# Seven products of quarters for the value projections of two mixers, in one place

## The chip, the cores and the metric

The kernel runs on one core of one Trainium2 chip. The metric is the device time of one execution in microseconds, the median of the timed runs. A core has TensorE (PE, matrix products; its loads of the stationary operand are listed as PEld), VectorE (DVE), ScalarE (ACT), GpSimd (POOL) and SyncE (SP). Each engine works through its own list of instructions in order, and the lists are tied together by semaphores: an instruction can wait until a semaphore has a value, and can raise one when it is done. SP, ACT and POOL also issue DMAs.

## The reference, cut to what matters

One layer of a decoder on 512 tokens of width 1024: a norm, one input projection `w_in`, four token mixers that run beside each other, a gated sum, an output projection, and a gated MLP. The part at issue is the projection of the normed x onto the values of two of the mixers, 512 columns each:

```
xn = rmsnorm(x, mix_norm_g[l])
p = xn @ w_in[l]
(aq, ak, av, ao, ai, af, bb, bc, bx, cz, cxbc, cdt,
 sq, sk, sv, gates) = jnp.split(p, SPLIT_POINTS, axis=-1)
ya = mlstm(aq, ak, av, ao, ...)
yd = stick_breaking_attention(sq, sk, sv)
```

So `[sv | av]` = xn (512 x 1024) times a matrix of 1024 x 1024. `sv` are the values of the stick-breaking attention (called D in the kernel, four heads), `av` those of the mLSTM (A, four heads). C is the Mamba-2 mixer, whose convolved input is `xbc`; B is the short convolution.

## The kernel before

**Precision.** Each product of two float32 matrices is made of three matmuls in the format fp32r: high by high, high by low, low by high. ACT makes the high part of a weight tile (`w_hi`, L862, a copy that rounds), DVE the low part (`w_lo`, L1262, source less high part). The same is done for activations (`xn_hi`, `xn_lo`).

**Units.** The weights come as a stream of units. A unit is one tile of 128 x 1024 floats (512 KB), and an ordinary one gives one output tile of 128 columns by 512 tokens: 8 steps over the inner dimension, 24 matmuls with 512 moving columns. SP loads unit u + 4 into `raw`, a ring of four, when `lo_ready` says that unit u's raw tile has been read. In ACT's list iteration u waits for the end of unit u on TensorE (`unit_done`) and makes `w_hi` of unit u + 4 first; then come the evacuation of unit u and the steps that other mixers hang on it. DVE's iteration u makes `w_lo` of unit u + 4 first, then the same. Since the lists are in order, whatever stands behind a wait is held with it.

**Order of units.** D's q (0 to 3) and k (4 to 7), D's values (`U_DV`, 8 to 11), the small gates (`U_SMALL` = 12), A's q and k (13 to 16), A's values (`U_AV`, 17 to 20), A's output gate (21 to 24), xbc of C (`U_XBC`, 25 to 32), gates and lifts (from `U_GL_D` = 33), z, B, and so on, then the output projection (from 97) and the MLP.

**The two value projections.** They are wanted with tokens on the partitions, so the x tile is the stationary operand and the weights move. D's values (L516) run in four units over four PSUM banks, 96 matmuls of 512 columns. A's values (L534) run in four units, half the columns at a time, 192 matmuls of 256 columns. DVE copies them to `dv` (L1332) and `av` (L1336).

**PSUM.** Eight banks, GB0 to 3 and X0 to 3. Units 4 to 7 go to X1, X2, X3, X0.

**The stick-breaking heads.** Head h starts at unit `D_AT[h]` = 12 + 4h. On TensorE: scores at that unit's end (L626), the suffix sums at the end of the third unit after (L652, waits for `sp_lo`), the product with the values at the fourth (L640). Between them DVE masks (L1437), ACT makes abs, exp and ln over 1280 columns (L985 to L987), DVE adds (L1442), ACT makes `sp_hi` (L991), DVE `sp_lo` (L1273); after the suffix DVE subtracts (L1419) and ACT makes exp (L961); after the product ACT makes `y_hi` (L978) and DVE `y_lo`, which raises `d_lo`.

**The mLSTM heads** start at unit 33 (`A_AT`). Their first scores (L671) wait for all four heads' `d_lo`.

**The xbc units.** ACT scales the tile into `stg` with the last tap (L926), DVE adds three taps (L1354), ACT makes the silu of the tile before (L933). In the sixth of them that silu waits for all sixteen `d_suffix`. Silu, exp/ln and sigmoid are in different tables, and a change of table is a load (L850).

**The start.** ACT makes the rstd of x by unit 2; POOL multiplies x_in by it (L415); ACT and DVE make `xn_hi` and `xn_lo`, with the gain folded in, beside units 3 to 6.

**The down projection** at the end already uses seven products of quarters, with the quarters' sums of its weights made by accumulating DMAs that POOL issues (L471), and the sums of its activations by DVE (L1711 to L1718).

Of the kernel before, what the change touches and what calls it, by code (L numbers as in the profile page):

```python
# [26 lines left out]
ALU = mybir.AluOpType  # L27
# [4 lines left out]
P = 128  # L32
# [36 lines left out]
PRODUCTS = ("P1", "P5", "P6", "P3", "P7", "P2", "P4")  # L69
# [7 lines left out]
C_T = 52  # L77
# [31 lines left out]
def build(nc, w_stream, w_quad, xT, vecs, rowsm, finrow, out_tok):  # L109
# [18 lines left out]
    bank_of = [o % 8 if o < 8 else o % 4 if o < 12 else o % 3 if o < first_tile[U_OUT] else (o + BANK0) % 4 for o in range(TILES0)]  # L128
# [129 lines left out]
    def low(name, offset):  # L258
# [14 lines left out]
    x1_turned = at("x1_turned", [P, KD, T], F32, TURNED)  # L273
    xg, st = at("xg", [P, NB, T], F32, base), f_ac
# [5 lines left out]
    Q11, Q12, Q21, Q22 = range(4)  # L280
    PLAIN_ORDER = (0, 1, 4, 5, 2, 3, 6, 7)
# [15 lines left out]
        dv_done d_scores d_masked d_soft_in d_soft d_sp_hi d_sp_lo d_suffix d_expo d_weights d_out d_hi d_lo  # L297
# [56 lines left out]
    def _(sp):  # L354
# [52 lines left out]
    def _(pool):  # L407
# [6 lines left out]
        for k in range(KD):  # L414
# [11 lines left out]
        pool.wait_ge(S["unit_done"], U_DV)  # L426
        pool.memset(negm[:], 0.0).then_inc(S["filled"], 1)
        pool.memset(g_x[:], 0.0).then_inc(S["masks"], 1)
        pool.memset(g_row[:], 0.0).then_inc(S["masks"], 1)
        pool.wait_ge(S["masks"], 5)  # L430
        pool.wait_ge(S["filled"], 4)
        pool.affine_select(out=negm[:], in_=negm[:], compare_op=ALU.is_ge, fill=NEG, base=-1,
                           pattern=[[1, T]], channel_multiplier=-1).then_inc(S["masks"], 1)
        pool.wait_ge(S["unit_done"], U_SMALL + 1)
# [45 lines left out]
    def _(pe):  # L480
# [23 lines left out]
        def unit(u):  # L504
# [3 lines left out]
            if U_DV <= u < U_DV + 4:  # L508

                part = u - U_DV  # L510
                for tb in range(NB):
                    if part == 0:
                        bank_free(o + tb)
                    for k in range(2):
                        for q, (x, w) in enumerate(((xn_hi, w_hi), (xn_lo, w_hi), (xn_hi, w_lo))):
                            ins = pe.matmul(GB[tb][:, :], x[:, 2 * part + k, tb * P:tb * P + P],  # L516
                                            w[:, u % RING, k * T:k * T + T], start=(part == 0 and k == 0 and q == 0),
                                            stop=(part == 3 and k == 1 and q == 2))
                    if part == 3 and tb < NB - 1:
                        ins.then_inc(S["dv_done"], 1)  # L520
                ins.then_inc(S["unit_done"], 1)
                return
            if U_AV <= u < U_AV + 4:


                half = (u - U_AV) % 2
                for tb in range(NB):
                    if half == 0 and tb % 2 == 0:
                        bank_free(o + tb // 2)
                    out = gb(o + tb // 2)[:, 256 * (tb % 2):256 * (tb % 2) + 256]  # L530
                    for k in range(4):
                        c = k * 256
                        for q, (x, w) in enumerate(((xn_hi, w_hi), (xn_lo, w_hi), (xn_hi, w_lo))):
                            ins = pe.matmul(out, x[:, 4 * half + k, tb * P:tb * P + P], w[:, u % RING, c:c + 256],  # L534
                                            start=(half == 0 and k == 0 and q == 0 and tb % 2 == 0),
                                            stop=(half == 1 and k == 3 and q == 2), skip_group_check=True)
                ins.then_inc(S["unit_done"], 1)
                return
# [46 lines left out]
        for u in range(U_OUT):  # L585
# [25 lines left out]
            if u == 22:  # L611
# [1334 lines left out]
```

## Time and profile before

| | us |
|---|---|
| median of 3 runs | 999.82 |
| lowest, highest | 999.6, 999.83 |
| profiled execution | 999.67 |
| its span | 997.9 |
| TensorE busy in it | 990.7 |
| DVE busy | 648.1 |
| ACT busy | 449.7 |
| POOL busy | 46.0 |

The profiled execution is one run; what lies outside its span is 1.8 us. A busy TensorE is made of matmuls that overlap: each row of a 512-column matmul lasts 0.39 us, but the next one starts earlier. So durations of stretches on TensorE are taken from start to start.

### The profile page before, as it was taken

The page shows a single profiled execution, that of the slowest core. Times are in us where ns is not written, and L with a number is a line of the kernel's source. Part 1 is how long each engine was busy: PE and PEld are TensorE (multiplying, and loading weights), DVE is VectorE, ACT ScalarE, POOL GpSimd, SP SyncE. Part 2 cuts the span into 40 slices and gives each one's busy share as a digit, 9 for nine tenths or more (in the row PEclk, how much of TensorE's full clock was granted, in tenths as well). Part 3 has the DMA queues.
Part 4 walks back from the last instruction along what each step waited for, and adds up shares of the span by engine and source line. Part 5 has one row for each costly group of instructions (what it writes and reads, how often), then busy time and mean ns, then how long its engine had stood idle before and what let it go on. Part 6 is the DMA issues. An engine that isn't in the chain of part 4 may idle for free.

```text
span 997.9 us, 12378 instructions
## 1 busy us (share of the span) xinstructions
PE 990.7 (99%) x4520; PEld 811.5 (81%) x4520; DVE 648.1 (65%) x869; ACT 449.7 (45%) x561; POOL 46.0 (5%) x64
## 2 busy tenths in 40 slices
PE   9999999999999999999999999999999999999997
PEld 7878988888787887777888888888888888888886
DVE  6836753757777566556463447767777777764775
ACT  7424455555645322444332334454444444442646
POOL 0610000000000000000000000000000000001210
PEclk9999999999999999999999999999999999999999
DMA  7332221223322343442252332274232232367942
GB/s 255 124 112 85 85 87 64 85 95 105 106 82 78 131 132 116 138 135 88 86 187 88 104 96 95 86 169 125 84 105 92 97 105 84 104 237 199 196 86 85
DMA packets 49002, 115.08 MB, mean 115 GB/s; under 512 B 20276, under 2 KB 21428, under 8 KB 48832
## 3 DMA queue, kind: packets, MB, share of 16 engines
q1 hardware_dynamic: 27072, 91.62, 27.3%
q0 software_dynamic: 5008, 20.51, 8.2%
q10 hardware_dynamic: 16880, 2.37, 1.5%
q8 instruction: 29, 0.48, 0.2%
q14 instruction: 13, 0.11, 0.0%
HBM read 110.24 MB, written 4.25 MB: 115 GB/s over the span
## 4 chain that ended last, share of the span: by engine, by line
PE 96%; DVE 1%; ACT 1%; issue 1%; DMA 0%; SPq 0%; ACTq 0%
PE gb L486 71%; PE xb L788 5%; PE gb L788 2%; PE xb L486 2%; PE gb L516 2%; PE gb L534 2%; PE gb L768 2%; PE xb L768 2%; PE xb L652 1%; PE gb L569 1%; PE xb L724 1%; PE xb L626 1%; PE gb L640 1%; PE xb L682 1%; PE gb L833 1%
## 5 line engine op out<-in xcount | busy, mean ns | idle before, releaser
L1262 DVE TENSOR_TENSOR w_lo<-raw,w_hi 128x1024 fp32r<-128x1024 f32 x152 | 189.3, 1245 | 208.1 <-ACT w_hi L862 207.6
L862 ACT ACTIVATE w_hi<-raw 128x1024 fp32r<-128x1024 f32 x153 | 161.9, 1058 | 323.4 <-PE gb L486 283.8
L486 PE MATMUL gb<-xn_hi,w_hi 128*128 128x512 f32 x720 | 282.0, 392 | 0.0
L486 PE MATMUL gb<-xn_hi,w_lo 128*128 128x512 f32 x720 | 280.3, 389 | 0.0
L486 PE MATMUL gb<-xn_lo,w_hi 128*128 128x512 f32 x720 | 280.2, 389 | 0.0
L486 PEld LDWEIGHTS gb<-xn_hi,w_hi 128*128 128x128 f32 x720 | 135.2, 188 | 28.4 <-issue 0.8
L486 PEld LDWEIGHTS gb<-xn_hi,w_lo 128*128 128x128 f32 x720 | 135.2, 188 | 28.4
L486 PEld LDWEIGHTS gb<-xn_lo,w_hi 128*128 128x128 f32 x720 | 135.3, 188 | 27.8 <-issue 0.2
L486 PE MATMUL gb<-y_hi,w_hi 128*128 128x512 f32 x352 | 138.4, 393 | 0.0
L486 PE MATMUL gb<-y_hi,w_lo 128*128 128x512 f32 x352 | 137.0, 389 | 0.0
L486 PE MATMUL gb<-y_lo,w_hi 128*128 128x512 f32 x352 | 137.0, 389 | 0.0
L486 PEld LDWEIGHTS gb<-y_hi,w_hi 128*128 128x128 f32 x352 | 66.1, 188 | 14.6 <-issue 0.9
L486 PEld LDWEIGHTS gb<-y_lo,w_hi 128*128 128x128 f32 x352 | 66.0, 188 | 14.2 <-issue 0.7
L486 PEld LDWEIGHTS gb<-y_hi,w_lo 128*128 128x128 f32 x352 | 66.1, 188 | 13.9
L850 ACT ACT_TABLE_LOAD x35 | 44.9, 1283 | 5.6 <-DVE t L1525 3.7
L1753 DVE TENSOR_TENSOR w_lo<-wr,w_hi 128x1024 fp32r<-128x1024 f32 x24 | 28.9, 1223 | 25.3 <-ACT w_hi L1179 25.3
L1179 ACT ACTIVATE w_hi<-wr 128x1024 fp32r<-128x1024 f32 x24 | 25.2, 1059 | 38.1 <-PE gb L768 15.6
L1128 ACT ACTIVATE f_cv<-f_sq,vec 128x512 f32<-128x512 f32 x40 | 32.4, 809 | 16.2 <-DVE f_sq L1691 16.2
L1691 DVE TENSOR_TENSOR f_sq<-gb,f_rs 128x512 f32<-128x512 f32 x40 | 27.6, 689 | 16.8 <-PE gb L486 16.1
L1697 DVE SCALAR_TENSOR_TENSOR f_cv<-f_sq,vec,f_cv 128x510 f32<-128x510 f32 x40 | 30.0, 750 | 6.1 <-DVE f_cv L1694 6.1
L1694 DVE SCALAR_TENSOR_TENSOR f_cv<-f_sq,vec,f_cv 128x511 f32<-128x511 f32 x40 | 29.9, 749 | 1.0
L1138 ACT ACTIVATE a_hi<-f_cv 128x256 f32 x16 | 6.7, 417 | 40.7 <-DVE f_cv L1702 40.7
(308 smaller groups left out, 1268.2 us busy)
## 6 DMA issues: line engine op xcount, KB each, us to landing
raw<-w_stream SPq DMA_DIRECT2D x153, 512.0 KB, 3.3
wr<-w_quad POOLq DMA_DIRECT2D x16, 512.0 KB, 7.3
abc<-scr_a POOLq DMA_DIRECT2D x8, 640.0 KB, 4.1
wr<-w_quad SPq DMA_DIRECT2D x8, 512.0 KB, 5.3
x_in<-xT SPq DMA_DIRECT2D x8, 256.0 KB, 5.4
x<-xT POOLq DMA_DIRECT2D x1, 2048.0 KB, 8.5
scr_x<-x_turned ACTq DMA_DIRECT2D x4, 512.0 KB, 5.7
x<-scr_x POOLq DMA_DIRECT2D x1, 2048.0 KB, 16.4
```

Of the source, the lines that this page charges most:

```text
L486: ins = pe.matmul(out, w[:, r, lo:hi], rhs(k)[x], start=(first and n == 0 and q == 0), stop=(last_ and n == len(ks) - 1 and q == 2))
L768: ins = pe.matmul(DOWN_PS[n][:, :], x[:, k, tt * P:tt * P + P], w[:, (U_DOWN + k) % RING, fh(h)], start=(k == 0 and q == 0), stop=(k == N_ ...
L788: ins = pe.matmul(ps[tau][:, :], x[:, p, tau * P:tau * P + P], w[:, r, fh(half)], start=(first and q == 0), stop=(last_ and q == 2), skip_ ...
L850: act.preload_act_table_set(name)
L862: act.activation(w_hi[:, r, 0:n], raw[:, r, 0:n], ACT.Copy).then_inc(S["hi_ready"], 1)
L1128: act.activation(f_cv[:, half, side, :], f_sq[:], ACT.Identity, bias=fcw[:, tile, 3:4], scale=fcw[:, tile, 2:3]).then_inc(S["f_tap"], 1)
L1179: act.activation(w_hi[:, u % RING, :], src, ACT.Copy).then_inc(S["hi_ready"], 1)
L1262: dve.tensor_tensor(w_lo[:, r, 0:n], raw[:, r, 0:n], w_hi[:, r, 0:n].bitcast(F32), ALU.subtract)\
L1691: dve.tensor_tensor(f_sq[:], ps[:, :], f_rs[:], ALU.mult).then_inc(S["psum_read_dve"], 1)
L1694: dve.scalar_tensor_tensor(out=w[:, 1:T], in0=f_sq[:, 0:T - 1], scalar=fcw[:, tile, 1:2], in1=w[:, 1:T], op0=ALU.mult, op1=ALU.add).then_i ...
L1697: dve.scalar_tensor_tensor(out=w[:, 2:T], in0=f_sq[:, 0:T - 2], scalar=fcw[:, tile, 0:1], in1=w[:, 2:T], op0=ALU.mult, op1=ALU.add).then_i ...
L1753: dve.tensor_tensor(w_lo[:, u % RING, :], source(name, j), w_hi[:, u % RING, :].bitcast(F32), ALU.subtract)\
```

## The change

It computes `[sv | av]` in one place, unit 8 on, as a product of two matrices cut into quarters (tokens 2 x 256, inner dimension 2 x 512, columns `sv` and `av`), with seven products of quarters where a plain one has eight. Each product is 24 matmuls with 512 moving columns and takes two units, so the section has 14 units (8 to 21), in the order P1, P2, P5, P3, P6, P7, P4.
- Weights: `wv` holds the first quarter and POOL adds others to it by three accumulating DMAs for each half; `wv2` likewise, once. P2's quarter comes through the ring. ACT and DVE make high and low parts for all 14.
- Activations: at the end of unit 7 ACT multiplies x_in by the gain, in eight pieces. DVE makes four sums (`v_a5`, `v_s2`, `v_s4`, `v_s3`, 128 x 1024 each), and ACT and DVE split each into high and low.
- Results: P1 stays in its banks, and P6, P7, P4 are added onto it there; ACT copies intermediate results to `dv` and `av`, and DVE adds or subtracts onto them.
- TensorE waits for DVE's read of unit 7 ahead of the section.
- The small gates become unit 22; w_small no longer carries the gain, as x_in does. A's values as units of their own are gone. The D heads start at 22, 26, 30, 34; xbc is 31 to 38; `U_GL_D` is 39. All later units move by six, with the same distances among them. The counts of semaphores that the down projection shares are raised, and SP's list is adapted.

The core of the diff; the first `values` is TensorE's, the gained x is in ACT's iteration 7, the second `values` is DVE's:

```diff
+V_PRODUCTS = ("P1", "P2", "P5", "P3", "P6", "P7", "P4")
+U_DQ, U_DK, U_V = 0, 4, 8
+U_SMALL = U_V + 2 * len(V_PRODUCTS)
+SKIP = U_SMALL - U_V - 2
+U_AQ, U_AK, U_AO, U_XBC = U_SMALL + 1, U_SMALL + 3, U_SMALL + 5, U_SMALL + 9
+U_GL_D = U_XBC + 8
-D_AT = [12 + 4 * h for h in range(D_HEADS)]
-A_AT = [33 + 4 * h for h in range(A_HEADS)]
+D_AT = [U_SMALL + 4 * h for h in range(D_HEADS)]
+A_AT = [U_GL_D + 4 * h for h in range(A_HEADS)]
...
+        def v_add(tile, j, q, name, sem):
+            pool.wait_ge(S["lo_ready"], V_OF[name] + j + 1)
+            pool.dma_start(tile[:, j, :], v_quad[q, j], accum_op=ALU.add).then_inc(S[f"{sem}{j}"], 16)
...
+        def values():
+            pe.wait_ge(S["xn_ready"], KD)
+            pe.wait_ge(S["psum_read_dve"], order[first_tile[U_V - 1]][1])
+            for name in V_PRODUCTS:
+                u = V_OF[name]
+                fresh = name in ("P1", "P2", "P5")
+                if name in ("P1", "P2", "P3"):
+                    if name == "P3":
+                        pe.wait_ge(S["s_lo"], 2)
+                    for j in range(2):
+                        pe.wait_ge(S["lo_ready"], u + j + 1)
+                        for tau in range(2):
+                            if name == "P3" and j == 0:
+                                pe.wait_ge(S["v_put"], 3 + tau)
+                            for kk in (2 * j, 2 * j + 1):
+                                ins = v_step(name, kk, tau, fresh and kk == 0, kk == 3)
+                        ins.then_inc(S["unit_done"], 1)
+                    continue
+                pe.wait_ge(S["s_lo"], {"P5": 1, "P6": 3, "P7": 4, "P4": 4}[name])
+                pe.wait_ge(S["lo_ready"], u + 1)
+                for tau in range(2):
+                    if name == "P6" and tau == 0:
+                        pe.wait_ge(S["v_put"], 2)
+                    elif name == "P7":
+                        pe.wait_ge(S["s_read"], 3 + tau)
+                    elif name == "P4":
+                        pe.wait_ge(S["s_read"], 5 + tau)
...
+            if u == U_V - 1:
+                act.wait_ge(S["xn_ready"], KD)
+                for k in range(KD):
+                    act.activation(x_in[:, k, :], x_in[:, k, :], ACT.Identity, scale=gain(V_MIX, k))\
+                        .then_inc(S["v_gained"], 1)
...
+        def values():
+            dve.wait_ge(S["v_gained"], KD)
+            dve.tensor_tensor(v_a5[:], xq(4, 1), xq(0, 1), ALU.subtract).then_inc(S["f_s2"], 1)
+            dve.wait_ge(S["f_s2"], 1)
+            dve.scalar_tensor_tensor(out=v_s2[:], in0=v_a5[:], scalar=-1.0, in1=xq(0, 0),
+                                     op0=ALU.mult, op1=ALU.subtract).then_inc(S["f_s2"], 1)
+            v_lo_of(12)
+            dve.wait_ge(S["f_s2"], 2)
+            dve.scalar_tensor_tensor(out=v_s4[:], in0=xq(4, 0), scalar=-1.0, in1=v_s2[:],
+                                     op0=ALU.mult, op1=ALU.subtract).then_inc(S["f_s2"], 1)
+            dve.tensor_tensor(v_s3[:], xq(0, 0), xq(0, 1), ALU.subtract).then_inc(S["f_s2"], 1)
+            v_lo_of(13)
+            v_split(0)
+            v_split(1)
+            v_lo_of(14)
+            v_split(2)
+            v_split(3)
+            dve.wait_ge(S["unit_done"], V_OF["P2"] + 2)
+            dve.wait_ge(S["v_put"], 2)
+            for tau in range(2):
+                dve.tensor_tensor(dv[:, tau, :], dv[:, tau, :], V_A[tau][:, :], ALU.add).then_inc(S["s_read"], 1)
+            for u in range(15, 20):
+                v_lo_of(u)
+            for tau in range(2):
+                dve.wait_ge(*((S["unit_done"], V_OF["P6"] + 2) if tau else (S["o_part"], 2)))
+                dve.wait_ge(S["v_put"], 5 + tau)
+                dve.scalar_tensor_tensor(out=av[:, tau, :], in0=V_B[tau][:, :], scalar=-1.0, in1=av[:, tau, :],
+                                         op0=ALU.mult, op1=ALU.subtract).then_inc(S["s_read"], 1)
...
```

ACT's list in the section, in words: `w_hi` of unit 12 after the gained x, `w_hi` 13, two copies of P1, the splits `v_h5` and `v_h4`, `w_hi` 14, the splits `v_h2` and `v_h3`, `w_hi` 15, the copy of P5's first half, `w_hi` 16, the copy of its second half, `w_hi` 17, `w_hi` 18 (waits for wv2's first half with its accumulating load), the copies of the masks, `w_hi` 19 (second half), the two copies of P3, `w_hi` 20 to 25 and the last two copies. Of the wv2 loads, POOL issues the first when `w_lo` 14 is done and the second when `w_lo` 15 is.

## Rows read from the trace of the kernel before

**Rows 1.** page: busy times, clock granted to TensorE, chain that ended last
```profile
PE 990.7 (99%) x4520; PEld 811.5 (81%) x4520; DVE 648.1 (65%) x869; ACT 449.7 (45%) x561; POOL 46.0 (5%) x64
PEclk9999999999999999999999999999999999999999
PE 96%; DVE 1%; ACT 1%; issue 1%; DMA 0%; SPq 0%; ACTq 0%
```

**Rows 2.** waits of TensorE: engine, line <- releaser: us, times, longest
```profile
PE xb L565 <- POOL cst L410: 1.1, 1, 1.1
```

**Rows 3.** timeline of TensorE (start, us, line, what): first values, behind them
```profile
51.24 0.39 PE L516 MATMUL gb<-w_hi,xn_hi 128*128 128x512 f32 x1
...
73.10 1.92 PE L555 MATMUL gb<-x_in,w_small 128*32 128x512 f32 x16
```

**Rows 4.** timeline of TensorE: the second mixer's values, 106 to 134 us
```profile
106.92 0.36 PE L534 MATMUL gb<-w_hi,xn_hi 128*128 128x256 f32 x1
...
124.65 0.40 PE L652 MATMUL xb<-sp_hi,tri_r 128*128 128x512 f32 x1
...
127.36 0.33 PE L534 MATMUL gb<-w_hi,xn_hi 128*128 128x256 f32 x1
...
133.16 1.67 PE L626 MATMUL xb<-dq,dk 128*128 128x512 f32 x4
```

**Rows 5.** timelines of ACT and DVE at the end of unit 7
```profile
51.44 1.06 ACT L862 ACTIVATE w_hi<-raw 128x1024 fp32r<-128x1024 f32 x1 [4.38 <-PE xb L486]
...
52.54 1.23 DVE L1262 TENSOR_TENSOR w_lo<-raw,w_hi 128x1024 fp32r<-128x1024 f32 x1 [1.57 <-ACT w_hi L862]
53.68 0.68 DVE L1325 TENSOR_TENSOR dk<-xb,stg 128x512 f32<-128x512 f32 x1
```

**Rows 6.** timelines: gained x on ACT; a quarter's piece, two splits, DVE
```profile
11.35 2.78 ACT L889 ACTIVATE y_hi<-x_in,vec 128x512 fp32r<-128x512 f32 x4
...
867.70 0.42 DVE L1714 SCALAR_TENSOR_TENSOR s<-a,f_cv 128x256 f32 x1
...
930.59 2.35 DVE L1273 TENSOR_TENSOR l<-s,h 128x1024 fp32r<-128x1024 f32 x2
```

**Rows 7.** accumulating loads by POOL, all sixteen: time to landing
```profile
DMA to landing us min/median/max: 5.2/7.3/9.7
```

**Rows 8.** the same, of the one issued at 902.3 us alone
```profile
DMA to landing us min/median/max: 5.5/5.5/5.5
```

**Rows 9.** TensorE: fourth head's scores, suffix, values; first mLSTM scores
```profile
162.55 2.32 PE L626 MATMUL xb<-dq,dk 128*128 128x512 f32 x8
...
183.24 0.39 PE L652 MATMUL xb<-sp_hi,tri_r 128*128 128x512 f32 x1
...
191.46 2.32 PE L640 MATMUL gb<-t,dv 128*128 128x512 f32 x8
...
220.94 0.48 PE L671 MATMUL xb<-aq,ak 64*128 64x256 f32 x1
```

**Rows 10.** timeline of DVE: sp_lo, subtraction, an xbc evacuation, y_lo
```profile
181.16 1.49 DVE L1273 TENSOR_TENSOR sp_lo<-t,sp_hi 128x1280 fp32r<-128x1280 f32 x1 [1.34 <-ACT sp_hi L991]
...
187.07 1.67 DVE L1419 TENSOR_TENSOR t<-t,xb 128x512 f32<-128x512 f32 x4
192.17 2.32 DVE L1354 SCALAR_TENSOR_TENSOR stg<-gb,vec,stg 128x511 f32<-128x511 f32 x3 [3.43 <-ACT stg L926]
...
197.76 0.68 DVE L1273 TENSOR_TENSOR y_lo<-gb,y_hi 128x512 fp32r<-128x512 f32 x1
```

**Rows 11.** timeline of ACT: softmax's first step; table load, tap, silu
```profile
168.98 1.27 ACT L985 ACTIVATE t<-t 128x1280 f32<-128x1280 f32 x1
...
190.07 1.28 ACT L850 ACT_TABLE_LOAD   x1
191.36 0.78 ACT L926 ACTIVATE stg<-gb,vec 128x512 f32<-128x512 f32 x1
192.04 0.62 ACT L933 ACTIVATE xbc<-stg 128x512 f32<-128x512 f32 x1
```

More of the change, by code:

```diff
@@ L273, in build, with v_op @@
     x1_turned = at("x1_turned", [P, KD, T], F32, TURNED)
+    wv = at("wv", [P, 2, 1024], F32, A0 + 6 * 4 * T)
+    wv2 = at("wv2", [P, 2, 1024], F32, C0)
+    def v_op(name, dt, offset):
+        return at(name, [P, 4, 2 * P], dt, offset)
+    T0_AT, Y0_AT, OP = G0 + 3 * 4 * 4 * T, G0 - 8 * 4 * T, 4 * 2 * P * 4
+    v_a5, v_s2 = v_op("v_a5", F32, T0_AT), v_op("v_s2", F32, T0_AT + OP)
+    v_s4, v_s3 = v_op("v_s4", F32, Y1 + 4 * 4 * T), v_op("v_s3", F32, Y1 + 4 * 4 * T + OP)
+    v_l5, v_l2 = v_op("v_l5", F32R, T0_AT), v_op("v_l2", F32R, T0_AT + OP)
+    v_l4, v_l3 = v_op("v_l4", F32R, Y1 + 4 * 4 * T), v_op("v_l3", F32R, Y1 + 4 * 4 * T + OP)
+    v_h5, v_h4, v_h2, v_h3 = (v_op(n, F32R, Y0_AT + q * OP) for q, n in enumerate(("v_h5", "v_h4", "v_h2", "v_h3")))
+    V_SPLIT = [(v_a5, v_h5, v_l5), (v_s4, v_h4, v_l4), (v_s2, v_h2, v_l2), (v_s3, v_h3, v_l3)]
     xg, st = at("xg", [P, NB, T], F32, base), f_ac
@@ L433, in _ @@
                            pattern=[[1, T]], channel_multiplier=-1).then_inc(S["masks"], 1)
+        for j in range(2):
+            v_add(wv, j, Q22, "P5", "wr_t")
+        for j in range(2):
+            v_add(wv2, j, Q12, "P3", "wr2_t")
+        for j in range(2):
+            v_add(wv, j, Q21, "P6", "wr_t")
+        pool.wait_ge(S["unit_done"], U_SMALL)
+        pool.memset(g_row[:], 0.0).then_inc(S["masks"], 1)
         pool.wait_ge(S["unit_done"], U_SMALL + 1)
@@ L507, in unit @@
             pe.wait_ge(S["lo_ready"], u + 1)
[L508 to L538, printed above, removed]
             for q in range(n):
@@ L1409, in _ @@
+        for u in range(U_OUT):
+            if U_V <= u < U_SMALL:
+                if u == U_V:
+                    values()
+                continue
+            if U_V - RING <= u < U_V:
+                v_lo_of(u + RING)
             elif u < U_OUT - 1:
@@ L1431, in _ @@
                 if h == 0:
[L1432 removed]
+                    dve.wait_ge(S["masks"], 5)
                 if h:
@@ L1865, in put @@
             stream[u + n] = slabs(w[:, n * width:(n + 1) * width])
-    def put_tokens(u, w):
-        for n in range(2):
-            s = slabs(w[:, 256 * n:256 * n + 256])
-            stream[u + 2 * n], stream[u + 2 * n + 1] = s[:, :1024], s[:, 1024:]
     put(U_DQ, sq); put(U_DK, sk);
-    for n in range(4):
-        stream[U_DV + n] = slabs(sv[256 * n:256 * n + 256])
+    both = (sv, av)
+    values = np.zeros((4, 2, P, 1024), np.float32)
+    for q in range(4):
+        for j in range(2):
+            k0 = 4 * (q // 2) + 2 * j
+            values[q, j] = slabs(both[q % 2][P * k0:P * k0 + 2 * P])
     small = np.zeros((D, P), np.float32)
```

301 lines of the change are left out of this document (201 added, 100 removed).

## The prediction

> **What bounds the kernel.** I read the page first: TensorE is busy for 990.7 of 997.9 us, and 96% of the chain that ended last is its matmuls [rows 1]. Of its waits for other engines the longest is 1.1 us, at the very start [rows 2]. So the time is the sum of TensorE's work, and every other engine counts only where TensorE would have to wait for it. A change is worth the TensorE time it removes less the stalls that it makes. Then I read the timeline of TensorE where the two value projections stand, and the timelines of DVE and ACT beside the steps that the change ties to them.
>
> **What is removed.** D's values run from 51.24 to 73.10: 21.86 us for 96 matmuls of 512 columns, so 0.2277 us each [rows 3]. A's values run from 106.92 to 133.16, with 2.71 us of another head's suffix matmuls between (124.65 to 127.36): 23.53 us for 192 matmuls of 256 columns [rows 4]. Together 45.39 us.
>
> **What is added on TensorE.** 7 products x 8 steps (4 tiles of the inner dimension, 2 of tokens) x 3 (high-high, high-low, low-high) = 168 matmuls of 512 columns, at 0.2277 us: 38.25 us. Without a stall the change would bring 7.1 us. Of that 5.5 come from the eighth product (24 x 0.2277), the rest from the 256-column form, which took more per column.
>
> **Stall 1, before P1.** The new code waits, ahead of all products, for DVE's read of unit 7, though P1 writes the banks of units 4 and 5. DVE's order is w_lo of unit 11 first, then the read; w_lo waits for w_hi, which ACT starts when unit 7 ends. Before, this ran beside D's values: w_hi at 51.44, w_lo 52.54, the read 53.68 to 54.36 [rows 5]. Now P1 starts at 54.42 in place of 51.24: 3.18 us. P1 then ends at 59.9 and P2 at 65.35, 24 matmuls or 5.46 us each.
>
> **Stall 2, before P5.** Its input is built from the gained x. ACT gains x only after w_hi of unit 11: from 52.40, eight pieces with 0.68 us between starts (four took 2.78), to 57.91 [rows 6]. DVE then does, in its order, v_a5, v_s2, w_lo 12, v_s4, v_s3, w_lo 13, v_l5: seven operations of 128x1024. Two such took 2.35 and so 1.15 each [rows 6], with 0.15 more where v_s2 waits for v_a5: v_l5 is there at 57.95 + 7 x 1.15 + 0.3 = 66.3. P5 waits 1.0 us, from 65.35 to 66.3. ACT's split of v_a5, 1.06 like a w_hi [rows 5], is done at 63.1 and hides. The new operations read x_in in four pieces of 256. If each piece cost as an operation of its own (0.42 in the down stage [rows 6], 1.7 for four), P5 would come 2 us later; a one-operation price is my value, as the split reads whole pieces too; below 1.15 nothing shows.
>
> **Behind P5.** P5 ends at 71.8, P3 at 77.2, P6 at 82.7, P7 at 88.2, P4 at 93.6. Against each stands: v_l4 at 67.4; the copy of P5's first half by ACT, 69.8; w_lo 15 at 73.2, needed at 74.4; w_lo 17 at 75.4. All in time. P7 has the least cover: it needs the first read of P6 by DVE, which is queued behind w_lo 19, behind w_hi 19, behind the accumulating load of wv2's second half. POOL issues that when w_lo 15 is done, at 73.2. The sixteen such loads of the down stage landed 5.2 to 9.7 us after their issue, 7.3 in the median [rows 7]; one that was alone took 5.5 [rows 8]. No plain load runs here (the ring's next slot waits for unit 22), and the two accumulating loads behind it come later, so I take 5.5: landed 78.7, w_hi 79.8, w_lo 81.0, read 81.7, needed 82.7. The end at 9.7 costs 3.2 us, below 6.5 it costs nothing. DVE's and ACT's other additions, the sel sums moved to the end of the section, and POOL's masks lie beside products and cost nothing.
> The section thus lasts 93.6 - 51.24 = 42.4 and gains 45.4 - 42.4 = 3.0 us.
>
> **What moves up.** The stick-breaking heads keep their distance of four units, but start nine units ahead of the first xbc unit (U_XBC) in place of thirteen. Before, only head 3 met xbc units, and its chain was already near TensorE's end of work: scores at 162.55, sp_lo done at 182.65, wanted at 183.24 [rows 9, 10]. Now head 2 has exactly this place, and head 3 follows four units on, between xbc units 3 and 7. I carry the times of before on (old unit 28 is new unit 34): scores of head 3 at T = 191.46.
> - DVE has an xbc evacuation and a w_lo ahead of the mask, which begins where y_lo began before, 197.76, and lasts as long as the subtraction, 1.7 [rows 10]; colT's copy now stands in this chain too and adds 0.2 net of the transposes that it waits for: 199.7. Before, softmax began at 168.98 and sp_lo ended at 182.65, 13.7 later [rows 10, 11]. Now 199.7 + 13.7 = 213.4. TensorE comes for it 20.7 after the scores, as before (162.55 to 183.24), at 212.1. Stall 3: 1.3 us.
> - Suffix (2.7) to 216.1. ACT, at xbc unit 5, now waits for the suffix of head 3 before a silu (before, it had long ended), and w_hi, DVE's w_lo and the subtraction, table load and exp come behind that: 0.2 + 0.6 + 1.0 + 1.2 + 1.7 + 1.3 = 6.0 [rows 5, 10, 11]. TensorE's unit 38 takes 5.5 (24 matmuls). Stall 4: 0.5 us.
> - A's first scores wait for y_lo of head 3. Before, that was done at 198.4 and A's scores stood at 220.94, with four units between [rows 9, 10]. Now y_lo is queued on DVE behind two xbc evacuations (2.3 each) and a w_lo, and on ACT behind table load, tap, w_hi, tap and two silus. From the exp's end: 1.3 + 0.8 + 2.3 + 1.15 + 2.3 + 0.6 + 0.5 + 0.65 = 9.6 [rows 10, 11], against 2.1 (weighted values, 2.32 less the tail that overlaps) + 5.5 (unit 39) on TensorE. Stall 5: 2.0 us.
> These are 3.8 us. Behind A's scores ACT and DVE stand to TensorE as before; all later units keep their distances.
>
> **The sum.** -3.0 + 3.8 = +0.8 on the profiled execution's 999.67, which lies 0.15 under the median of the timed runs: 1000.6.
>
> **The clock.** TensorE was granted its upper level, 2.4 GHz, in every slice, and no wait behind the start is as long as 1 us [rows 1, 2]. Stall 1 would be its first of 3 us, so the cost of an idle TensorE shows in no row. If one product's matmuls ran at the lower level, 1.2 GHz, they would take twice as long, 5.5 us more, of which stall 2's 1.0 absorbs a part: +4.5.
> The Trainium skill (TensorE: Matmul & The Clock Gate, Part 1) says that the array's clock is halved after idle time and given back only under sustained work. By that rule the sum could be 1005; by the trace, which has no such gap, it is 1000.6. No run here shows it yet.
>
> **Rivals.**
> 1. Forecast: both effects as worked out, 999 to 1001.8. Chance 0.53.
> 2. Heads hide: head 3's chain fits after all, stalls 3 to 5 vanish. For it: I assume that no step overlaps better than its queue order. Against: the A wait is explicit and its chain is built of rows. It decides at y_lo before the end of unit 39. 1000.6 - 3.8 = 996.8. Chance 0.13.
> 3. Slower, accumulating loads: late landing before P7. Landing over 6.5 us starts to count; 9.7 gives 1000.6 + 3.2 = 1003.8, the median 7.3 gives 1001.4. For: three loads are issued within 2.3 us. Against: the first of them is the one that counts. Chance 0.16.
> 4. Slower, the clock falls in stall 1: 1000.6 + 4.5 = 1005.1. Chance 0.08.
> 5. The change does only what it says, and no new wait is seen: 999.8 - 7.1 = 992.7. Against: stall 1 can't be covered by the order of DVE's work. Chance 0.04.
> The rest, 0.06, are stalls that I have not seen, on the slow side.
>
> **How the numbers follow.** Under 0.2% (2 us) a measurement of this kernel can't tell from no change. Under 997.8 lie rival 5 and nearly all of rival 2: 0.16. Over 1001.8 lie rival 4, most of rival 3, the unseen stalls and a little of the forecast: 0.30. Between: 0.54. The range takes in rival 2 and most of rival 3, 996.5 to 1003.5; outside are rivals 4 and 5 and the tail of 3, about 0.18.
>
> **What would show it.** In the profile after: TensorE idle for about 3 us at 51 with the read of unit 7 behind it; P5 waiting for v_l5 by 1 us; small product at about 93.5; the xb matmuls of A's first scores waiting for y_lo by 2 us. A lower clock in the slice at 51, or w_hi waiting for wv2's load near 79 for over 2 us, would show rivals 4 and 3. The prediction is wrong in its ground if the sum of TensorE's idle time grows by less than 5 us or more than 11.

## The result, and the profile after

The changed kernel takes 1001.9 us in the median of ten runs (1001.03 to 1003.59), the kernel before, run between them on the same chip, 999.83 (999.38 to 1000.04). The ratio is 1.0022, with a 95% interval of 1.0013 to 1.0032. It is slower, by about the 0.2% that the forecast took as the least that can be told from no change. I had forecast 1000.6, with 0.54 on no change to be seen and 0.30 on slower. The size is off by 1.3 us. The mechanism of the forecast is there, but one of its rivals came true beside it.

The profiled execution took 1001.6 us, its span is 1000.1. From the page after, the lines that answer to [rows 1]: busy times, granted clock in 40 slices of 25 us, and the chain.

```profile
PE 985.9 (99%) x4400; PEld 802.0 (80%) x4400; DVE 663.2 (66%) x881; ACT 476.9 (48%) x593; POOL 52.1 (5%) x72
PEclk9999999999999999999999999999999999999999
PE 90%; DVE 4%; ACT 3%; issue 2%; DMA 1%; SPq 0%; ACTq 0%; DVEq 0%
```

TensorE runs 120 matmuls fewer, 4400 for 4520, as the change says. Its busy time falls by only 4.8 us where the sum had 7.1 of work less, and its time outside of work rises from 7.2 to 14.2 (span less busy). The chain now passes through DVE and ACT for 7% of the span, where [rows 1] had 2%: work of theirs sets TensorE's end in some places. The clock's slices are too coarse to show a fall of a few microseconds: each still reads 9. The five longest waits of TensorE in the kernel after (engine, operation and line, releaser: us, times, longest) name the places:

```profile
PE xb L594 <- issue: 3.4, 1, 3.4
PE xb L744 <- issue: 1.8, 1, 1.8
PE xb L636 <- POOL cst L443: 1.1, 1, 1.1
PE xb L725 <- DVE sp_lo L1413: 1.1, 1, 1.1
PE gb L713 <- ACT t L1101: 0.4, 1, 0.4
```

The third is the wait at the start, there before [rows 2]. The other four are stalls 1, 5, 3 and 4 of the prediction, in this order. Stall 2, P5 behind v_l5, isn't there. A wait in this view is counted from the modelled end of the matmul before, 0.16 us after the next could have started (0.39 long at a pitch of 0.23), so each of them moves the work behind it by 0.16 more than it says.

**The products.** TensorE's timeline in the kernel after, at the first matmuls of P1, one in its middle, the last slow ones, then the first of P2, of P5, and the small product (start, length, line; the bracket is the idle time before):

```profile
54.70 0.47 PE L594 MATMUL xb<-w_hi,xn_hi 128*128 128x512 f32 x1 [3.39 <-issue]
55.01 0.39 PE L594 MATMUL xb<-w_lo,xn_hi 128*128 128x512 f32 x1
...
57.45 0.63 PE L594 MATMUL xb<-w_hi,xn_lo 128*128 128x512 f32 x1
57.87 0.63 PE L594 MATMUL xb<-w_hi,xn_hi 128*128 128x512 f32 x1
...
61.86 0.39 PE L594 MATMUL gb<-w_hi,xn_hi 128*128 128x512 f32 x1
...
67.30 0.39 PE L594 MATMUL xb<-w_hi,v_h 128*128 128x512 f32 x1
...
94.59 0.64 PE L569 MATMUL gb<-x_in,w_small 128*32 128x512 f32 x4
```

P1 starts 3.46 us after the place where D's values began [rows 3]; 3.18 was forecast. P2 takes 5.44 us (61.86 to 67.30), as any product should, but P1 takes 7.16. In its middle the matmuls stand 0.42 to 0.43 us apart in place of 0.23 and last 0.63 in place of 0.39. The windows of 1 us over P1 say why; the columns are the length, the busy time of PE, PEld, DVE, ACT and POOL, the clock granted to TensorE, the DMA share and GB/s:

```profile
54.00:55.00 1.00, 0.30 (x1) 0.30 (x2) 0.60 (x1) 1.00 (x3) 0.00 (x0) 1.00 0.03 12
55.00:56.00 1.00, 1.00 (x5) 0.82 (x4) 0.00 (x0) 1.00 (x2) 0.00 (x0) 0.82 0.90 254
56.00:57.00 1.00, 1.00 (x3) 0.73 (x3) 0.00 (x0) 1.00 (x3) 0.00 (x0) 0.50 0.69 274
57.00:58.00 1.00, 1.00 (x4) 0.79 (x3) 0.62 (x1) 0.35 (x1) 0.00 (x0) 0.50 0.00 0
58.00:59.00 1.00, 1.00 (x4) 0.81 (x3) 0.97 (x2) 0.00 (x0) 0.00 (x0) 0.50 0.00 0
59.00:60.00 1.00, 1.00 (x5) 0.80 (x5) 0.87 (x1) 0.68 (x1) 0.00 (x0) 0.97 0.00 0
```

The clock fell from 2.4 GHz to 1.2 (0.50) about 0.9 us after P1 had started behind the gap of 3.4 us, and stayed there for some 3.4 us of TensorE's work. The clock withheld is 0.18 + 3 x 0.50 + 0.03 = 1.71 us, and P1 is longer by 7.16 - 5.46 = 1.70. The Trainium skill (TensorE: Matmul & The Clock Gate, Part 1) says that the clock is halved after idle time and comes back under sustained work; this trace agrees.

**What led to P1 and P5.** The timelines of ACT, DVE and POOL in the kernel after, from unit 7's end:

```profile
52.36 4.99 ACT L1113 ACTIVATE x_in<-x_in,vec 128x512 f32<-128x512 f32 x8
...
52.48 1.52 DVE L1538 TENSOR_TENSOR w_lo<-raw,w_hi 128x1024 fp32r<-128x1024 f32 x1 [1.62 <-ACT w_hi L1038]
53.92 0.68 DVE L1465 TENSOR_TENSOR dk<-xb,stg 128x512 f32<-128x512 f32 x1
57.38 1.23 DVE L1551 TENSOR_TENSOR v_a<-x_in 128x1024 f32<-128x1024 f32 x1 [2.78 <-ACT x_in L1113]
...
60.41 1.23 DVE L1538 TENSOR_TENSOR w_lo<-wv,w_hi 128x1024 fp32r<-128x1024 f32 x1 [0.54 <-ACT w_hi L1038]
...
65.07 1.23 DVE L1413 TENSOR_TENSOR v_l<-v_a,v_h 128x1024 fp32r<-128x1024 f32 x1
...
52.32 0.60 POOL L469 TENSOR_SCALAR_AFFINE_SELECT negm<-negm 128x512 f32<-128x512 f32 x1
```

The read of unit 7 ends at 54.60, 0.10 before P1: "issue" in the list of waits is this read. The w_lo before it took 1.52 us where [rows 5] had 1.23, and POOL's select (52.32 to 52.92) runs beside its first third. The eight gains took 4.99 us, from 52.36 to 57.35, where I had counted 5.5 by [rows 6]. v_a5 starts 0.6 us earlier than I had it, at 57.38, as one operation of 1.23 us. The 0.54 ahead of w_lo 12 is a wait that the forecast didn't have: ACT makes w_hi 12 when the first half of P1 is done, and that half ran at the low clock. So v_l5 is done at 66.30.

**The heads.** DVE at sp_lo and y_lo of head 3, ACT at its exp and at the silu before, TensorE at its scores, its suffix, its product with the values, and A's first scores, all of after:

```profile
182.49 2.32 PE L699 MATMUL xb<-dq,dk 128*128 128x512 f32 x8
...
202.87 1.49 DVE L1413 TENSOR_TENSOR sp_lo<-t,sp_hi 128x1280 fp32r<-128x1280 f32 x1 [1.34 <-ACT sp_hi L1132]
...
204.41 0.50 PE L725 MATMUL xb<-sp_hi,tri_r 128*128 128x512 f32 x1 [1.07 <-DVE sp_lo L1413]
...
207.43 0.63 ACT L1008 ACTIVATE xbc<-stg 128x512 f32<-128x512 f32 x1 [2.99 <-PE xb L725]
...
211.90 1.27 ACT L1101 ACTIVATE t<-t 128x1280 f32<-128x1280 f32 x1 [1.58 <-DVE t L1614]
...
213.31 1.10 PE L713 MATMUL gb<-t,dv 128*128 128x512 f32 x2 [0.40 <-ACT t L1101]
...
222.15 0.69 DVE L1413 TENSOR_TENSOR y_lo<-gb,y_hi 128x512 fp32r<-128x512 f32 x1 [1.18 <-ACT y_hi L1119]
...
222.94 0.45 PE L744 MATMUL xb<-aq,ak 64*128 64x256 f32 x1 [1.78 <-issue]
```

Each of the three places is the one that the prediction named. y_lo ends at 222.84, and A's scores come 0.10 later. From the small product to A's first scores lie 128.35 us; before, less A's values, it was 220.94 - 73.10 - 23.53 = 124.31 [rows 3, 4, 9]. The heads thus cost 4.04 us. The small product stands at 94.59, where it would be at 73.10 + 23.53 = 96.63 with both projections ahead of it: the section gains 2.04. A's first scores are 2.00 us late, by both kernels' timelines (222.94 to 220.94), and what lies behind them adds little: the whole kernel is 2.1 us later by the medians and 2.2 by the spans.

### The profile page after: what moved, and what is told of

It reads as the page before. It is cut to its first block, busy times and chain, and to the rows that moved or that the text cites. A ratio compares the mean times of both kernels' runs of the same rounds, so it can differ in the third digit from the quotient of the medians.

```text
span 1000.1 us, 12193 instructions
## 1 busy us (share of the span) xinstructions
PE 985.9 (99%) x4400; PEld 802.0 (80%) x4400; DVE 663.2 (66%) x881; ACT 476.9 (48%) x593; POOL 52.1 (5%) x72
## 4 chain that ended last, share of the span: by engine, by line
PE 90%; DVE 4%; ACT 3%; issue 2%; DMA 1%; SPq 0%; ACTq 0%; DVEq 0%
PE gb L531 67%; PE xb L861 5%; PE xb L594 3%; PE gb L861 2%; PE xb L531 2%; PE gb L841 2%; PE xb L841 2%; DVE stg L1482 1%; PE xb L797 1%; PE xb L725 1%; ACT L923 1%; PE gb L640 1%; PE gb L713 1%; PE xb L699 1%; PE xb L755 1%
## 5 line engine op out<-in xcount | busy, mean ns | idle before, releaser
L1403 DVE TENSOR_TENSOR w_lo<-raw,w_hi 128x1024 fp32r<-128x1024 f32 x144 | 178.4, 1239 | 183.4 <-ACT w_hi L937 182.9
L937 ACT ACTIVATE w_hi<-raw 128x1024 fp32r<-128x1024 f32 x145 | 153.4, 1058 | 279.7 <-PE gb L531 269.4
```

The costliest lines, as they stand in the source:

```text
L937: act.activation(w_hi[:, r, 0:n], raw[:, r, 0:n], ACT.Copy).then_inc(S["hi_ready"], 1)
L1403: dve.tensor_tensor(w_lo[:, r, 0:n], raw[:, r, 0:n], w_hi[:, r, 0:n].bitcast(F32), ALU.subtract)\
```

## The experiments

All kernels of a block ran on one chip between runs of the kernel before, whose medians there were 999.78 (kernels 1 to 4), 999.73 (5 to 8) and 999.75 us (9 to 12).

**1 and 2. Gaps of two lengths put into the kernel before.** They ask whether the clock falls by the gap alone, and from what length it does. Nothing of the change is in them, and the computation is the same. Ahead of D's values, where before there is no wait, TensorE waits for DVE's read of unit 7 (b_read7), or for DVE's w_lo of unit 11, which is one operation earlier (b_wlo11).

```diff
             if u == U_DV:
                 pe.wait_ge(S["xn_ready"], KD)
+                pe.wait_ge(S["psum_read_dve"], order[first_tile[U_DV - 1]][1])   # b_read7
+                pe.wait_ge(S["lo_ready"], U_DV + 4)                              # b_wlo11
```

> The kernel before with one added wait: TensorE waits for DVE's read of unit 7 ahead of D's values, as the changed kernel does, and nothing else of the change. Queue and clock theory: TensorE is idle for 3.2 to 3.4 us at 51, its granted clock then falls to the lower level for about 3.5 us as in the changed kernel (1.7 us of work lost), and nothing absorbs either: 999.8 + 3.3 + 1.7 = 1004.8. Queue theory without a clock (the slow matmuls of P1 belong to the new products or to the loads beside them): clock stays up, 1003.1.

> The kernel before with a shorter added wait: TensorE waits for w_lo of unit 11 (done at 53.8) ahead of D's values. If any idle time of a few us lets the clock fall: idle 2.6 us and 1.7 lost, 1004.1. If this gap is too short for it: 999.8 + 2.6 = 1002.4, and the clock stays at its upper level.

b_read7: 1004.35 us (1004.20 to 1004.58), ratio 1.0044 (1.0028 to 1.0061). b_wlo11: 1002.56 (1002.08 to 1004.23), ratio 1.0031 (1.0020 to 1.0041). The wait and the windows of b_read7, then those of b_wlo11:

```profile
PE gb L516 <- issue: 3.1, 1, 3.1
...
54.00:56.00 2.00, 1.67 (x4) 1.41 (x5) 0.23 (x1) 0.00 (x0) 0.10 (x1) 0.55 0.61 180
56.00:58.00 2.00, 2.00 (x6) 1.54 (x6) 0.00 (x0) 0.00 (x0) 0.00 (x0) 0.59 0.23 90
```

```profile
PE gb L516 <- issue: 2.5, 1, 2.5
...
53.00:55.00 2.00, 1.26 (x6) 1.08 (x7) 1.24 (x2) 0.00 (x0) 1.11 (x1) 1.00 0.15 31
55.00:57.00 2.00, 2.00 (x10) 1.66 (x9) 0.00 (x0) 0.00 (x0) 0.00 (x0) 1.00 0.66 231
```

By the medians the gap of 3.1 us costs 4.57 us. In its profile the first matmul of D's values stands at 54.34, 3.10 later than before, and the small product at 77.86, so the values take 23.52 us in place of 21.86: 1.66 more, with the clock low. The gap of 2.5 us costs 2.78 by the medians; in its profile the values start 2.49 later (53.73) and take 21.98, 0.12 more, with the clock full. So the gap brings the fall without anything of the change beside it. The shorter one isn't quite safe: seven of its nine runs are at 1002.08 to 1002.63, two at 1004.07 and 1004.23. Those two are longer by what a fall costs, and their mean granted clocks are the lowest of the nine, 0.997 against 0.998 and 0.999.

**3. The wait for unit 7 moved ahead of P5 (a_wait_late).** P1 writes the banks of units 4 and 5, so it doesn't need the read of unit 7; the wait put in its place is for the read of unit 6. P5 is the first that writes unit 7's bank.

```diff
-            pe.wait_ge(S["psum_read_dve"], order[first_tile[U_V - 1]][1])
+            pe.wait_ge(S["psum_read_dve"], order[first_tile[U_V - 2]][1])
             for name in V_PRODUCTS:
+                if name == "P5":
+                    pe.wait_ge(S["psum_read_dve"], order[first_tile[U_V - 1]][1])
```

> The changed kernel, with TensorE's wait for the read of unit 7 put ahead of P5, the first product that writes that bank; P1 waits only for the reads of the banks it writes. Stall 1 goes. Queue theory: P5 still can't start before v_l5 at 66.3, so the idle time moves there (62.1 to 66.3). With the clock theory the fall moves with it and P5 takes 1.7 longer, where P5 now starts at 67.3 at full clock: 1001.9 - 1.0 + 1.7 = 1002.6. Without a clock effect of idle time: 1000.9. If stall 1 were a loss of its own: 1001.9 - 5 = 997.

1001.9 us (1000.48 to 1003.26), ratio 1.0019 (1.0010 to 1.0029): no gain at all. The first matmul of P5 and the windows behind it:

```profile
65.84 0.47 PE L594 MATMUL xb<-w_hi,v_h 128*128 128x512 f32 x1 [3.45 <-issue]
...
66.00:68.00 2.00, 2.00 (x7) 1.52 (x7) 2.00 (x3) 1.21 (x2) 0.00 (x0) 0.62 0.76 131
68.00:70.00 2.00, 2.00 (x6) 1.60 (x5) 2.00 (x3) 0.00 (x0) 0.85 (x1) 0.53 1.00 170
```

P1 starts at once, at 51.32, and P2 ends at 62.2, but P5's input, v_l5, is done only at 65.74 (66.30 in after), so the same 3.4 us of waiting stand ahead of P5, and the clock falls there too (0.62, 0.53). The stall has moved, and it took the clock's price with it.

**4. Six of the eight gains one iteration of ACT earlier (a_gain_early).** ACT makes them at unit 6, and only two behind w_hi of unit 11.

```diff
-            if u == U_V - 1:
-                act.wait_ge(S["xn_ready"], KD)
-                for k in range(KD):
+            if u in (U_V - 2, U_V - 1):
+                act.wait_ge(S["xn_ready"], 6 if u == U_V - 2 else KD)
+                for k in (range(6) if u == U_V - 2 else range(6, KD)):
```

> The changed kernel, with six of the eight gained pieces of x one iteration earlier in ACT's list, so that v_a5 can start 3 us earlier. Stall 1 stays. Queue and clock theory: P5 starts at 67.3 because P2 ends then, not because of v_l5, so nothing changes: 1001.9. Theory that the chain over the gained x bounds the section: P5 starts up to 3 us earlier, 999.

1002.01 us (999.93 to 1003.35), ratio 1.0023 (1.0014 to 1.0033). Alone it brings nothing: P5 follows P2 without a wait, as it already does in after. Its ten runs show the clock's part by themselves. Two are at 999.93 and 1000.70, four at 1001.80 to 1002.04, four at 1003.04 to 1003.35, and their mean granted clocks are 0.998, 0.997 and 0.996 in these three groups.

**5. Both (a_front).** The edits of 3 and 4 together.

> The changed kernel with both edits: the wait for the read of unit 7 ahead of P5, and six gained pieces of x one iteration earlier. Queue and clock theory: P1 starts at 51.2, no gap is long enough for the clock to fall, v_l5 is done at 62.6 and P5 starts then in place of 67.3: 1001.9 - 4.6 = 997.3, and the spread of the runs is as small as before. If another step takes over (the loads before P7, DVE's list), less: 999.

997.6 us (997.06 to 997.95), ratio 0.9979 (0.9969 to 0.9989): 4.3 us under the changed kernel. One wait is left in the section:

```profile
63.11 0.47 PE L594 MATMUL xb<-w_hi,v_h 128*128 128x512 f32 x1 [0.57 <-issue]
```

The clock is 1.00 throughout, the small product stands at 90.49 in place of 94.59, and the runs lie within 0.9 us, where those of after spread over 2.6. Neither edit alone brings anything: with the first P5 waits for its late input, with the second P1 still waits for unit 7, and each wait has the full length. Together they take 4.1 us out of the section, of the 5.2 that stall 1 (3.46) and its clock (1.70) had put in; P5's wait of 0.6 is part of what stays.

**6 to 8. The chain of head 3.** In a_mask_first DVE masks head 3 ahead of the xbc evacuation of that iteration; in a_y_first ACT's y_hi and DVE's y_lo of head 3 stand ahead of theirs; a_heads has both. In the old places head 3 is left out (`D_AT[:3]`).

```diff
+            if s - 1 == D_AT[3]:                          # a_mask_first, DVE
+                dve.wait_ge(S["d_weights"], 3)
+                for j in range(NB):
+                    dve.wait_ge(S["d_scores"], NB * 3 + j + 1)
+                    ins = dve.tensor_tensor(t0[:, blk(j)], X[j][:, 0:BLK_W[j]], negm[:, 0:BLK_W[j]], ALU.add)
+                ins.then_inc(S["d_masked"], 1)
             evac(u)
...
+            if s - 5 == D_AT[3]:                          # a_y_first, ACT; DVE's y_lo in the same way
+                act.wait_ge(S["d_out"], 4)
+                act.activation(y_hi[0][:, 3, :], GB[3][:, :], ACT.Copy).then_inc(S["d_hi"], 1)
             evac(u)
```

> The changed kernel; in DVE's iteration 34 the mask of head 3 stands ahead of the evacuation of the xbc unit. Queue theory: softmax starts 1.9 us earlier, sp_lo is in time, stall 3 (1.1 us) goes, stalls 4 and 5 stay, since both count from the suffix: 1001.9 - 1.1 = 1000.8. If it only moves the wait to the next step: 1001.9.

> The changed kernel; in iteration 38 ACT's y_hi and DVE's y_lo of head 3 stand ahead of the evacuation of the xbc unit. Queue theory: y_lo is done at 219.3, before unit 39 ends, stall 5 (1.8 us) goes: 1001.9 - 1.8 = 1000.1. If A's first head then waits for its own steps instead (they come 1.2 us later in both lists): up to 1001.9.

> Both edits of the heads. Queue theory: stalls 3 and 5 go, stall 4 (0.4) stays: 1001.9 - 2.9 = 999.0. If they cover for each other: 1000.

a_mask_first: 1000.96 us (1000.23 to 1002.27), ratio 1.0014. Its list of waits has lost sp_lo; the 1.7 at A's scores and the 0.4 at the exp are still there. a_y_first: 1000.13 (998.45 to 1001.35), ratio 1.0004; the wait at A's scores is gone and sp_lo's is still there. a_heads: 998.73 (996.93 to 1000.05), ratio 0.9989 (0.9979 to 0.9998). From the changed kernel's 1001.9 that is 0.9, 1.8 and 3.2 less. All three kernels kept stall 1 and its spread of 2 to 3 us, so these medians alone don't show whether the two gains add exactly (0.9 and 1.8 against 3.2). Kernel 9 measures the pair without that spread: it is 3.2 under kernel 5, which has no fall of the clock (997.6 to 994.42). So the two were worth 3.2 of the 4.0 us that the heads cost. In a_y_first's profile the low clock lasted longer:

```profile
56.00:58.00 2.00, 2.00 (x6) 1.57 (x5) 0.27 (x1) 1.70 (x3) 0.00 (x0) 0.50 0.55 213
58.00:60.00 2.00, 2.00 (x6) 1.52 (x6) 1.97 (x2) 0.00 (x0) 0.00 (x0) 0.50 0.00 0
60.00:62.00 2.00, 2.00 (x9) 1.60 (x8) 0.58 (x2) 1.06 (x1) 0.00 (x0) 0.76 0.00 0
```

There P1 took 8.30 us (55.05 to 63.35), 2.8 over its 5.46. In the other profiles of the changed kernel with this gap (after and kernels 4, 6, 8 and 11) it took 7.11 to 7.17. One gap has more than one price. In windows of 0.25 us the eight profiles with such a gap show why: the clock is low for 3.4 us in seven of them and for 6.8 in a_y_first, and this stretch begins 0.9 us before the first matmul behind the gap in a_y_first, 0.1 before it in b_read7, 0.9 behind it in after and 1.4 behind it in a_gain_early. Only the part that TensorE works through is paid.

**9. All of it (a_all).** a_front and a_heads together.

> The changed kernel with the four edits tried so far: the wait for the read of unit 7 ahead of P5, six gained pieces earlier, mask of head 3 and y of head 3 ahead of the xbc evacuations. Queue and clock theory: the front edits (-4.3 measured) and the head edits (-3.2 measured) add, as they touch stretches that don't meet: 994.4, and the clock stays up. If they cover for each other: 997.

994.42 us (994.30 to 994.84), ratio 0.9948 (0.9934 to 0.9961). 4.3 and 3.2 off 1001.9 make 994.4: the gains of the front and of the heads add up, as they must if the two groups of stalls have nothing to do with each other.

**10. The gap filled (a_fill).** To part the clock from the waiting, the changed kernel gets 12 matmuls of 512 columns ahead of P1. They compute nothing that is used: P1 overwrites their result. They wait for the reads up to unit 6 and not for that of unit 7.

```diff
+            pe.wait_ge(S["psum_read_dve"], order[first_tile[U_V - 2]][1])
+            pe.wait_ge(S["lo_ready"], U_V + 1)
+            for n in range(12):
+                pe.matmul(V_B[0][:, :], xn_hi[:, n % 4, 0:P], w_hi[:, U_V % RING, 0:HALF], start=(n == 0),
+                          stop=(n == 11), skip_group_check=True)
             pe.wait_ge(S["psum_read_dve"], order[first_tile[U_V - 1]][1])
```

> The changed kernel; ahead of its wait for the read of unit 7 TensorE makes twelve matmuls of 512 columns (2.7 us) whose result is overwritten by P1. The wait ends as before, so only the idle time goes. Clock theory: the clock stays up, P2 ends 1.7 us earlier, at 65.6, and P5 then waits for v_l5 at 66.3: 1001.9 - 1.0 = 1000.9, with a spread as small as before. If the slow matmuls of P1 had another cause: 1001.9.

1000.28 us (1000.11 to 1000.76), ratio 1.0007 (0.9997 to 1.0016). TensorE at the start of P1, P2 and P5, and DVE at v_l5:

```profile
54.72 0.50 PE L594 MATMUL xb<-w_hi,xn_hi 128*128 128x512 f32 x1 [0.61 <-DVE dk L1470]
...
60.33 0.39 PE L594 MATMUL gb<-w_hi,xn_hi 128*128 128x512 f32 x1
...
65.77 0.40 PE L594 MATMUL xb<-w_hi,v_h 128*128 128x512 f32 x1
...
64.40 1.22 DVE L1418 TENSOR_TENSOR v_l<-v_a,v_h 128x1024 fp32r<-128x1024 f32 x1
```

P1 starts at the same time as in after, 54.72 to 54.70, and the profile now names the read for which it waits. It takes 5.61 us in place of 7.16, the granted clock is 1.00 in all windows over it, and the kernel is 1.6 us faster with a spread of 0.65 us. This is the clock's price, shown alone: useless work in a gap makes the kernel faster. It also came out under what I had expected, since P5 doesn't wait: v_l5 is done at 65.62, 0.15 before P2 ends. With P1 where it starts in after, stall 2 would not have been there at the full clock either. The margin is thin: had P1 started at 54.42, as forecast, and taken 5.46, P2 would have ended at 65.34 and P5 would have waited about 0.3 us (an estimate from these rows).

**11. POOL's select out of w_lo's way (a_pool_later).** Two more fills on POOL let its select start late in the w_lo of unit 11, and not ahead of it. Timed once.

```diff
         pool.wait_ge(S["unit_done"], U_V)
+        pool.memset(g_sp[:], 0.0).then_inc(S["filled"], 1)
+        pool.memset(g_ab[:], 0.0).then_inc(S["filled"], 1)
         pool.memset(negm[:], 0.0).then_inc(S["filled"], 1)
         pool.memset(g_x[:], 0.0).then_inc(S["masks"], 1)
-        pool.wait_ge(S["filled"], 4)
+        pool.wait_ge(S["filled"], 6)
```

> The changed kernel; POOL makes two more memsets (1 us) ahead of its affine select, which then stands beside DVE's read of unit 7 as in the kernel before, not beside w_lo of unit 11. Theory that the select held w_lo (1.52 in place of 1.23): w_lo 1.23, stall 1 shorter by 0.3, time the same within what can be measured. If something else held it: w_lo stays at 1.52.

1001.71 us. w_lo on DVE, and the select on POOL; the last line is the select in the kernel before:

```profile
52.94 1.23 DVE L1540 TENSOR_TENSOR w_lo<-raw,w_hi 128x1024 fp32r<-128x1024 f32 x1 [1.60 <-ACT w_hi L1040]
...
53.70 0.93 POOL L471 TENSOR_SCALAR_AFFINE_SELECT negm<-negm 128x512 f32<-128x512 f32 x1
...
53.06 1.18 POOL L432 TENSOR_SCALAR_AFFINE_SELECT negm<-negm 128x512 f32<-128x512 f32 x1
```

w_lo takes 1.23 us again, though fills run beside it, and the wait ahead of P1 is 3.1 in place of 3.4. Now it is the select, second to start, that is the longer one, 0.93 us for 0.60. The kernel before had shown the same: there POOL made three fills ahead of its select, which began in the midst of w_lo (52.54 to 53.77) and took 1.18, while w_lo took 1.23. The change put one of the fills, that of g_row, behind the section, and so the select ahead of w_lo. So the fills take nothing from DVE, and of w_lo and select the later one is held up. The Trainium skill (SBUF — State Buffer, Who interferes with whom) has DVE's second read port shared with GpSimd: an instruction of DVE with two inputs, such as w_lo, meets one of GpSimd that reads. Select and fill behave so here. That it is the port is the word of the Trainium skill; the runs show only who is slowed beside whom.

**12. The best of the order (a_best).** a_all, and besides: DVE subtracts head 3 ahead of the w_lo of that iteration, and w_lo 13 and v_l5 stand ahead of v_s4 and v_s3, as does ACT's split of v_a5 ahead of its copies of `dv`.

```diff
             if u == V_OF["P1"] + 1:
+                v_split(0)
                 for tau in range(2):
                     v_copy(dv[:, tau, :], V_B[tau], "unit_done", V_OF["P1"] + 2)
-                v_split(0)
...
             v_lo_of(12)
+            v_lo_of(13)
+            v_split(0)
...
+            if u + 1 - 4 == D_AT[3]:
+                for j in range(NB):
+                    dve.wait_ge(S["d_suffix"], NB * 3 + j + 1)
+                    ins = dve.tensor_tensor(t0[:, blk(j)], t0[:, blk(j)], X[j][:, 0:BLK_W[j]], ALU.subtract)
...
```

> As the kernel with four edits, and two more: DVE subtracts head 3's suffix ahead of w_lo 41 (against stall 4, 0.4 us), and v_l5 is made ahead of v_s4 and v_s3 (against the 0.6 us that P5 still waited). Queue theory: 994.4 - 1.0 = 993.4; TensorE's waits behind the start under 1.5 us in all. If the next wait is close behind: 994.4.

993.18 us (992.76 to 993.45), ratio 0.9933 (0.9920 to 0.9947): 6.6 us faster than before and 8.7 faster than the change as it was made. All of TensorE's waits of 0.3 us and more in it:

```profile
PE xb L638 <- POOL cst L443: 1.1, 1, 1.1
PE gb L642 <- ACT y_hi L966: 0.6, 1, 0.6
PE xb L760 <- DVE s_lo L1418: 0.3, 1, 0.3
```

Of the 7.1 us of matmul work that the change removes, 6.6 now reach the time, and TensorE's busy time is 984.0 us, 6.7 under that of the kernel before. That agrees with the first two terms of the sum, 45.39 removed and 38.25 added.

## Why the prediction came out as it did

**TensorE's work, right.** 120 matmuls fewer, a product 5.44 us, and 6.6 of the 7.1 us once most of the stalls are gone.

**Stall 1, right in place and cause, 0.3 short.** 3.18 forecast, 3.46 measured. The step that was missing is POOL's: I had the masks on POOL cost nothing because I looked only for who waits for them, not for whom they run beside. The change brings the select forward, ahead of w_lo. Kernel 11 gives back 0.3 of the wait, and its one run shows no gain in the whole time (1001.71).

**The clock, the term that failed.** I gave the fall a chance of 0.08 because no row showed a gap of this size. A missing row was no ground for a low chance: the trace of before has no wait behind the start of even 1 us, so it said nothing at all about one of 3. Kernels 1 and 10 show the fall from two sides. Rival 4's size was wrong the other way: 4.5 us, as I let the whole product run at 1.2 GHz, where the clock came back after some 3.4 us. It costs 1.7 in the profile of after and 1.6 by kernel 10. That the measured time lay near the forecast is in part luck: the 1.7 of the clock was partly set off by the 1.0 of a stall 2 that didn't come.

**Stall 2, wrong.** 1.0 forecast, none measured. In the kernel after, P1's 1.7 us at the low clock would have covered it, but kernel 10 shows v_l5 0.15 us in time without that. The mis-sized term is the gain of x: eight in 4.99 us, where [rows 6] priced a form with another output format at 0.68 each. The chain of v_a5 to v_l5 behind it takes 8.17 us in kernel 10 (57.45 to 65.62), where 8.35 was forecast for seven operations. In after it takes 8.92, with the wait of 0.54 for w_hi 12, so that v_l5 ends at 66.30, the very time that was forecast. That is luck: a start 0.6 too early and a wait that wasn't foreseen.

These three terms make the section: +0.28 for the wait, +1.70 for the clock, -0.97 for stall 2, so that the small product stands at 94.59 where 93.6 was forecast, and the gain is 2.0 instead of 3.0.

**P7's cover, right.** The page prices the accumulating loads of the value weights at 5.4 us in the median, with 5.5 assumed. In the timeline of ACT, w_hi 19 starts at 78.99, released by the load that POOL issued at 73.46, forecast 78.7; DVE's read of P6 starts at 81.23, and P7 has no wait. Rival 3 fell with this.

**Stalls 3 to 5, right.** Forecast 1.3, 0.5 and 2.0, together 3.8. By the starts of the matmuls around them they moved the work by 1.34 (202.95 to 204.75 less two pitches), 0.55 (212.53 to 213.31 less one) and 1.94 us (1.78 and the 0.16 of the view), together 3.8; the whole stretch lost 4.0. The chains were as long as summed: from head 3's scores to sp_lo's end 21.87 us (182.49 to 204.36) where 21.9 was forecast, and from the exp's end to y_lo's 9.67 (213.17 to 222.84) where 9.6 was. Kernels 6 and 7 took away the causes that the prediction named, the xbc evacuation ahead of the mask and those ahead of y_lo, and the waits went with them. Rival 2, heads that hide, fell, and rival 5 with it.

**The sum.** Forecast -3.0 + 3.8 = +0.8; measured -2.0 + 4.0 = +2.0. Of the difference, 1.0 is the clock and stall 1 less stall 2, and 0.2 the heads. The ground of the prediction, 5 to 11 us more of idle TensorE, held at 7.0. The range held the time, but the forecast's own interval, to 1001.8, did not.

What stays open: why one gap of about 3.4 us costs nothing in one run, 1.7 us in most and 2.8 in others. The runs show the spread, that it goes with the granted clock, and in the profiles where the low stretch begins and how long it is; they don't show what decides either, and the run at no cost (999.93 in kernel 4) is known by its time alone. Nor do they tell how little waiting is harmless; the wait of 1.8 us ahead of A's scores left the clock at 1.00 in the windows behind it in after, one of 2.5 cost two runs of nine a fall by their times, and nothing between was tried.

## What to carry to other kernels

When a change on the bounding engine removes work, list first what that engine will newly wait for, and price a wait of some microseconds at the wait and the clock behind it, even where the trace of before has no such gap. Give a wait its narrowest condition, and then ask what is late next: two late inputs for the same product have to be moved together, since either alone brings nothing. When a dependent chain moves into a stretch where its engines are busier, put its few short operations ahead of the long ones of each in-order list; here such moves, with the two edits of the front, turned 2 us lost into 6.6 gained.

## What I had not expected of the hardware

- A gap of 3.1 to 3.5 us in TensorE's work brought its clock from 2.4 to 1.2 GHz in the profile of every kernel that had one unfilled; it stayed there for 3.4 us in seven profiles and for 6.8 in one, and began anywhere from 0.9 us before TensorE's work went on to 1.4 after. The usual price was 1.6 to 1.7 us beside the wait. After 2.5 us it fell in the profile of none, and by their times in two runs of nine.
- The kernels with such a gap spread over 2 to 3.5 us (after 1001.03 to 1003.59, kernel 4 999.93 to 1003.35), those changed kernels without it over 0.9 or less. b_read7, with four runs within 0.4, is the exception.
- Twelve matmuls whose result nobody reads, put into the gap, made the kernel 1.6 us faster.
- An operation of DVE with two inputs from SBUF, 1.23 us, took 1.52 when POOL's select had started before it, and 1.23 beside POOL's fills. When it had started first, the select took 0.93 and 1.18 in place of 0.60.
